# Block sums kept in PSUM, the gate's convolution in two PSUM banks, and another order of the FFN's units

## What is computed

```python
def causal_dwconv(u, buf, w, b):
    L, W = u.shape[1], w.shape[0]
    full = jnp.concatenate([buf.astype(u.dtype), u], axis=1)
    out = b + sum(full[:, j:j + L] * w[j] for j in range(W))
    return out, full[:, L:]

def conv_ffn(xn, buf, w_up, cw, cb, w_down):       # D_MODEL 1024, D_FF 2816, width 3
    up = xn @ w_up                                 # 1024 -> 5632, values and gates
    upc, new_buf = causal_dwconv(up, buf, cw, cb)
    val, gate = jnp.split(upc, 2, axis=-1)
    return (jax.nn.gelu(gate) * val) @ w_down, new_buf
```

## Time and profile before

| | |
|---|---|
| median of 3 runs | 1179.66 us (1179.26 to 1181.84) |
| the profiled execution's own time | 1180.18 us |
| its span, first to last instruction | 1178.4 us |
| TensorE busy | 1062.7 us, 90% |
| VectorE busy | 829.4 us, 70% |
| ScalarE busy | 519.5 us, 44% |
| GpSimd busy | 500.5 us, 42% |
| mean granted TensorE clock | 0.943 of full speed |
| pairs 0 to 4, without D | about 625 to 722 us |
| pairs 5 to 20, with D and D' | about 722 to 1110 us |

### The profile page before, as it was taken

One profiled execution on the slowest core, in us unless ns is written; L12 is line 12 of the kernel. 1 busy time (PEld: TensorE's weight loads), 2 busy tenths in 40 slices (PEclk: granted clock), 3 DMA queues, 4 the chain that ended last, 5 costly groups with the idle time before them and its releaser, 6 DMA issues.

```text
span 1178.4 us, 19870 instructions
## 1 busy us (share of the span) xinstructions
PE 1062.7 (90%) x7688; PEld 1031.2 (88%) x7688; DVE 829.4 (70%) x1258; ACT 519.5 (44%) x869; POOL 500.5 (42%) x320
## 2 busy tenths in 40 slices
PE   8999999999999999999997876888878887888885
PEld 8899999999999999999986866888878887888885
DVE  6885569565664648464567898877787788787964
ACT  6577873143435343242344444343433444344453
POOL 4243333432232323223444556555554565455630
PEclk9999999999999999999997988888988999898998
DMA  8533323775968677453311231222121222223036
GB/s 207 167 83 94 94 73 99 179 198 129 249 147 237 155 188 214 154 198 116 108 54 37 72 90 57 61 79 75 54 63 55 72 81 55 62 68 85 23 88 195
DMA packets 263267, 132.94 MB, mean 113 GB/s; under 512 B 82720, under 2 KB 257045, under 8 KB 262920
## 3 DMA queue, kind: packets, MB, share of 16 engines
q1 hardware_dynamic: 262966, 131.63, 41.2%
q10 hardware_dynamic: 210, 0.07, 0.0%
HBM read 104.17 MB, written 25.29 MB: 110 GB/s over the span
## 4 chain that ended last, share of the span: by engine, by line
PE 56%; DVE 15%; issue 10%; DMA 9%; ACT 4%; POOL 4%; SPq 1%; DVEq 0%; POOLq 0%; ACTq 0%
PE ring L2630 35%; PE ring L3035 8%; DMA f_stage<-in_w_up 8%; DVE conv L1781 5%; PE bank L3021 3%; DVE gl L2527 2%; PE bank L2872 2%; POOL f_lo L1192 2%; POOL wlo L1151 2%; DVE f_stage L2358 2%; ACT f_hi L1586 2%; DVE f_stage L2359 1%; PE bank L2676 1%; DVE f_stage L2366 1%; ACT gh L1682 1%
## 5 line engine op out<-in xcount | busy, mean ns | idle before, releaser
L1151 POOL TENSOR_TENSOR wlo<-stage,whi 128x1024 fp32r<-128x1024 f32 x78 | 200.3, 2568 | 400.1 <-ACT whi L1205 400.1
L2630 PE MATMUL ring<-x_split,whi 128*128 128x322 f32 (+2 forms) x1952 | 347.5, 300 | 0.0
L1192 POOL TENSOR_TENSOR f_lo<-f_stage,f_hi 128x512 fp32r<-128x512 f32 x154 | 224.9, 1469 | 212.8 <-ACT f_hi L1586 211.7
L2630 PEld LDWEIGHTS ring<-x_split,whi 128*128 128x128 f32 x1952 | 294.4, 189 | 8.9 <-issue 8.1
L2630 PE MATMUL ring<-x_split,wlo 128*128 128x256 f32 (+1 forms) x976 | 210.4, 297 | 0.0
L1586 ACT ACTIVATE f_hi<-f_stage 128x512 fp32r<-128x512 f32 x154 | 94.7, 627 | 208.1 <-DVE f_stage L2366 90.9
L2630 PEld LDWEIGHTS ring<-x_split,wlo 128*128 128x128 f32 x976 | 164.6, 189 | 0.0
L3035 PE MATMUL ring<-gh,f_hi 128*128 128x280 f32 (+1 forms) x316 | 84.2, 354 | 69.3 <-DVE resid L2532 59.1
L3035 PEld LDWEIGHTS ring<-gh,f_hi 128*128 128x128 f32 x316 | 63.9, 236 | 74.5 <-DVE resid L2532 62.9
L1205 ACT ACTIVATE whi<-stage 128x1024 fp32r<-128x1024 f32 x79 | 83.3, 1054 | 81.5 <-PE ring L2630 70.6
L3021 PE MATMUL bank<-fx_T,f_hi 128*128 128x290 f32 x308 | 96.5, 313 | 22.3 <-ACT sum_one L1645 11.8
(11 more groups left out here) (423 smaller groups left out, 2266.6 us busy)
## 6 DMA issues: line engine op xcount, KB each, us to landing
stage<-in_w_in SPq DMA_DIRECT2D x56, 512.0 KB, 4.2
f_stage<-in_w_up SPq DMA_DIRECT2D x44, 512.0 KB, 5.2
d_stage<-in_w_down SPq DMA_DIRECT2D x40, 256.0 KB, 2.8
stage<-in_w_branch_a SPq DMA_DIRECT2D x8, 512.0 KB, 3.6
c_sample<-in_state_mlstm_C SPq DMA_DIRECT2D x16, 256.0 KB, 6.6
out_s_mlstm_C<-c_sample SPq DMA_DIRECT2D x16, 256.0 KB, 2.4
stage<-in_w_branch_b SPq DMA_DIRECT2D x8, 512.0 KB, 3.7
stage<-in_w_out SPq DMA_DIRECT2D x8, 512.0 KB, 3.6
```

The costliest lines, as they stand in the source:

```text
L1151: pool.tensor_tensor(spaced(wlo[:, slot]), packed(stage[:, slot, 0:n]), spaced(whi[:, slot]).bitcast(F32), ALU.subtract).then_inc(w_lo, 1)
L1192: pool.tensor_tensor(in_blocks(flo[n % RING], key), packed(piece(key)), in_blocks(fhi[n % RING], key).bitcast(F32), ALU.subtract).then_inc ...
L2630: last = pe.matmul(of(z, t0 or -2, t1), w[:, kk * WS:kk * WS + P], x_, start=kk == 0 and m == 0, stop=kk == kn - 1 and m == 2)
```

## The change

**Sums in place.** The sums of partial products are no longer made in SBUF tiles: VectorE adds the SBUF copy of one part onto the PSUM accumulator of the other and scales from there. A pair uses four banks for its accumulators (one of two alternating banks A for B11, T2, T3, T4; one bank B for B21; one bank C for T1 and B22), with no double buffering of B and C.

**Gate in PSUM.** The gate's convolution, its gelu and the product with the values stand in the two banks that this frees (`cv[1]`, `sample_product`); the values' convolution stays in SBUF (`val_taps`). The hi and lo parts of the product are each made by two instructions (512 and 64 columns).

**History.** The copy of the samples' history into `up` moves from VectorE to ScalarE (`history`).

**Order.** TensorE's units, and with them all the other engines' work, stand in another order; the product of pair i-1 is made in pass i and no longer pair i-2's. D and D' share `wide[1]` as before.

```diff
 def weight_order():
     for i in range(NPAIR):
         yield "B11", i
-        yield "B21", i
+        yield "T1", i
+        if d:
+            yield "D", *d
         if i:
             yield "T4", i - 1
-        if d:
-            yield "D", *d
         yield "T2", i
-        if i:
-            yield "B22", i - 1
-        yield "T1", i
+        yield "B21", i
+        yield "B22", i
         if d:
             yield "D", d[0], d[1] + 1
         yield "T3", i
...
-        acc_banks = ((bank[:, 0], bank[:, 1], bank[:, 2]), (bank[:, 3], ring[:, 0, 0], ring[:, 0, 1]))
+        pool_ = bank[:, :, :].rearrange("p h t -> p (h t)")
+        cv = (val_taps[:, 0:CV_N], pool_[:, 0:CV_N])
+        sample_product = pool_[:, CV_N:CV_N + TD - SEQ]
+        acc_a = (bank[:, 2, 0:QT], bank[:, 3, 0:QT])
+        acc_b, acc_c = ring[:, 0, 0, 0:QT], ring[:, 0, 1, 0:QT]
...
             def load_pair(i):
                 if i >= 2:
-                    sp.wait_ge(piece_split, split_done("B22", i - 2))
+                    sp.wait_ge(piece_split, split_done("T4", i - 2))
...
+            def history(i, j):
+                act.activation(grouped(up[:, j, US0:UW_F - UG], UG)[:, :, 0:FW - 1], hist[:, :, ft:ft + UPT + 1:UPT], ACT.Copy
...
-            def first_sum(i):
-                tt(s_one[:, 0:QS], s_one[:, 0:QS], acc(i, 1)[:, 0:QS], ALU.add).then_inc(c11_added, 1)
-            def first_scaled(i):
-                tt(up[:, 0, 0:QS], s_one[:, 0:QS], rbc[:, 0:QS], ALU.mult).then_inc(c11_scaled, 1)
+            def sum_one_one(i):
+                b = acc(i, "B21")[:, 0:QS]
+                tt(b, s_one[:, 0:QS], b, ALU.add).then_inc(sum_added, 1)
+                tt(up[:, 0, 0:QS], b, rbc[:, 0:QS], ALU.mult).then_inc(sum_scaled, 1)
+            def sum_one_two(i):
+                c = acc(i, "B22")[:, 0:QS]
+                tt(c, s_two[:, 0:QS], c, ALU.add).then_inc(sum_added, 1)
+                tt(up[:, 1, 0:QS], c, rbc[:, 0:QS], ALU.mult).then_inc(sum_scaled, 1)
+            def sum_two_two(i):
+                tt(b, s_five[:, :], acc(i, "T3"), ALU.add).then_inc(sum_added, 1)
+                second_half(i, 1, b)
...
             def product(i):
-                st(tt(grouped(pr[:, SEQ:TD], LS), grouped(cv[:, 0, US0:US0 + UG * NB], UG)[:, :, 0:LS],
-                tt(pr[:, 0:SEQ], cv[:, 0, 0:SEQ], cv[:, 1, 0:SEQ], ALU.mult).then_inc(prod_done, 1)
+                st(tt(grouped(sample_product, LS), sample_conv(val_taps[:, :]), sample_conv(cv[1]), ALU.mult))
+                tt(cv[1][:, 0:SEQ], cv[0][:, 0:SEQ], cv[1][:, 0:SEQ], ALU.mult).then_inc(prod_done, 1)
...
             for i in range(NPAIR):
-                if i >= 2:
-                    product(i - 2)
+                if before:
+                    down_evict(before[0], before[1] + 1)
...
-                    pe.wait_ge(c21_scaled, i - 1)
-                up_product("B11", i, 0)
+                    pe.wait_ge(sum_scaled, scaled(i - 2, "C21"))
+                up_product("B11", i, True)
+                    pe.wait_ge(sum_scaled, scaled(i - 1, "C12"))
+                up_product("T1", i, True)
+                    pe.wait_ge(sum_added, added(i - 1, "C22"))
+                    up_product("T4", i - 1, False)
                 pe.wait_ge(part_copied, parts(i, 1))
+                    pe.wait_ge(sum_scaled, scaled(i - 1, "C22"))
+                up_product("B21", i, True)
+                pe.wait_ge(part_copied, parts(i, 2))
+                up_product("B22", i, False)
```

More of the change, by code:

```diff
@@ L290, in parts, with added, scaled @@
     return 3 * i + n
+def added(i, block):
+    return 3 * i + {"C11": 1, "C12": 2, "C22": 3}[block]
+def scaled(i, block):
+    return 4 * i + {"C11": 1, "C12": 2, "C22": 3, "C21": 4}[block]
 class Chain:
@@ L490, in hybrid_layer @@
         up = sb("up", [P, 2, UW_F], r)
[L491 to L497, removed]
+        r += 8 * UW_F
+        s_one, s_two, s_five = sb("sum_one", [P, QT], r), sb("sum_two", [P, QT], r + 1184), sb("part_five", [P, QT], r + 2 * 1184)
+        r += 3 * 1184
+        val_taps = sb("val_taps", [P, CV_N + 4], r)
+        r += 4 * CV_N + 5888
         dst = [sb(f"d_stage{s}", [P, QN], r + 4 * QN * s) for s in range(2)]
@@ L1654, in third_part, with part_five @@
-            def third_part(i):
-                act.wait_ge(tile_done, unit_done("T3", i))
+                    act.wait_ge(sum_added, added(i - 1, "C11"))
+                act.activation(s_one[:, 0:QS], acc(i, "B11")[:, 0:QS], ACT.Copy).then_inc(part_copied, 1)
+            def part_five(i):
+                act.wait_ge(tile_done, unit_done("T1", i))
+                if i:
+                    act.wait_ge(sum_added, added(i - 1, "C22"))
+                act.activation(s_five[:, :], acc(i, "T1"), ACT.Copy).then_inc(part_copied, 1)
@@ L1722, in _ @@
             i, g0, g1 = NPAIR - 1, GROUPS - 2, GROUPS - 1
+            first_tap(i, 1)
             ahead("D", g0, 0)
-            product_hi(i - 1)
+            gelu(i)
             ahead("T4", i)
             first_tap(i, 0)
-            ahead("B22", i)
-            first_tap(i, 1)
             ahead("D", g0, 1)
-            gelu(i)
             ahead("D", g0, 2)
@@ new lines, in second_half @@
+            def second_half(i, j, z):
+                st(tt(up[:, j, QS:US0], z[:, 0:UH_F], rtwo[:, 0:UH_F], ALU.mult))
+                ins = tt(sample_rows(up[:, j])[:, :, FW - 1:], grouped(z[:, UH_F:QT], LS), grouped(rtwo[:, UH_F:QT], LS),
+                         ALU.mult)
+                ins.then_inc(sum_scaled, 1)
+                dve.wait_ge(sum_scaled, scaled(i, "C22" if j else "C21"))
+                last_rows(i, j)
+            def sum_two_two(i):
+                b = acc(i, "B21")
+                dve.wait_ge(part_copied, parts(i, 2))
+                dve.wait_ge(tile_done, unit_done("T3", i))
+                dve.wait_ge(sum_scaled, scaled(i, "C12"))
+                tt(b, s_five[:, :], acc(i, "T3"), ALU.add).then_inc(sum_added, 1)
+                dve.wait_ge(sum_added, added(i, "C22"))
+                second_half(i, 1, b)
@@ L3079, in _ @@
             down_product(g0, 0)
-            pe.wait_ge(part_copied, parts(i, 3))
-            up_product("T4", i, 0, False)
-            pe.wait_ge(c22_added, i + 1)
-            up_product("B22", i, 2, False)
-            pe.wait_ge(c21_scaled, i)
-            pe.wait_ge(c11_added, i)
+            pe.wait_ge(sum_added, added(i, "C22"))
+            up_product("T4", i, False)
+            pe.wait_ge(sum_scaled, scaled(i, "C22"))
             down_product(g0, 1)
-            pe.wait_ge(c11_added, i + 1)
-            pe.wait_ge(c12_added, i + 1)
+            pe.wait_ge(sum_scaled, scaled(i, "C21"))
             down_product(g0, 2)
```

213 lines of the change are left out of this document (88 added, 125 removed).

## The result

The changed kernel takes 1109.53 us (median of 4 runs, 1107.44 to 1112.07) against 1179.61 before: ratio 0.9403, 95% interval 0.9379 to 0.9427. That is 70 us less; the forecast was 109 us less (1071).

A forecast was written before the change was run, and what follows sets the result against it. It took VectorE's late eviction of D, stalling TensorE, as the bound. 16 pairs from 24.0 to 18.0 us save 96, five others 13: 109 off 1180.2 gives 1071 us, range 1050 to 1122.

The forecast's parts named there:

- the half clock of D': TensorE's D' unit, slowed to clock 0.50 behind its stall for the eviction, up to 2.6 us; expected back at full clock.
- Four banks are enough: PSUM accumulators of a pair: loops through single banks take less than 17.7 us, so no bank holds TensorE up.
- writing PSUM: Rival, chance 0.06 for slower: seven VectorE instructions per pair write PSUM dearly; 1143 us at a doubling, 1215 at 1.2 each.
- VectorE's two waits for a split piece: VectorE idle in front of 2389 (1.2 us) and 2396 (about 0.4) until GpSimd has split a piece: 1.6 per pair.
- Weights come in time: The next pair's weight loads, issued at 13.6 us, make about 20, when VectorE wants them at 19.8.
- the waits for GpSimd grow: In VectorE's pass, waits for GpSimd go from 2.0 to 2.7 us per pair, plus 0.6 for the fourth weight sum.
- The upper bound of 6.3: Six VectorE instructions reading two SBUF tiles each wait out most of a GpSimd operation: 20.8 us per pair, 1129 us.
- the lock fills what was freed: Rival, chance 0.15: VectorE's two-SBUF-input instructions and GpSimd's exclude each other; pass 19.5 to 20.8 us, 1102 to 1129.
- the case that carried the forecast: Pairs with D take 17.7 to 19.5 us, 1052 to 1102 us in all; chance 0.70, 0.20 of it TensorE alone.
- The rival of the clock: Rival, chance 0.06: stalls of 3.4 to 3.9 us at T1 bring clock 0.5 behind them; 22.8 us per pair, 1161 us.
- 6.0 each, 90: Saving in the pairs with D: each goes from 24.0 to 18.0 us.
- The list of savings, mean by mean: VectorE work removed per pair, from old mean durations: scaling, product, lo part and history, 4.9 of 19.1 us.

The follow-up runs named there:

- lo_zero: The changed kernel with GpSimd writing zeros for the lo parts of the FFN weights instead of subtracting two SBUF tiles: 1047.23 us.
- round_product: The changed kernel with ScalarE's hi part of the product moved behind the roundings of the next pair's T2, B21 and B22: 1063.33 us.
- sums_sbuf: The changed kernel with the three sums back in SBUF tiles, and C11, C12 and half of C22 scaled from two SBUF tiles: 1121.05 us.
- before_lo_zero: The kernel before the change, with GpSimd writing zeros for the lo parts of the FFN weights: 1090.14 us.
- order_alone: The changed kernel with sums, gate and product back in SBUF and the history copied by VectorE, keeping the new order: 1133.37 us.

## Why the prediction was right, and where its size was off

**Right.** The eviction is no longer what TensorE waits for; the half clock of D' is gone (some of it now stands behind T1); what is left stands before T1, on 2496. Four banks are enough: where VectorE is not the bound (lo_zero, round_product) TensorE has no gap, so no wait for a bank costs anything. Operands in PSUM take the times of their like, and writing PSUM costs next to nothing: the three sums take 449, 456 and 455 ns into PSUM, and 441, 446 and 446 into SBUF (sums_sbuf). VectorE's two waits for a split piece came nearly as worked out: 1.4 and 0.4 us per pair, 1.8 against the 1.6 of the sum. (The 1.3 of GpSimd in that sum is not in the earlier trace rows, whose mean is 1.46; the changed kernel's trace has 1.31 at 845.91.) Weights come in time.

**The mis-sized term** is "the waits for GpSimd grow": 2.0 scaled with GpSimd's busy share to 2.7, and 0.6 for 2396, 3.3 together. Measured from the rows above: 0.97 on 2396, 1.10 on 2381 and on 2382, 1.02 on 2389 and twice 0.97 on the values' taps make 6.1. The pass closes with it: 12.5 bare with handovers, 1.8 of waits and 6.1 of lock are 20.4. A busy share says how often an engine is found at work by one that comes at random; here both engines are released by the same few events, have several instructions queued, and take turns until one queue is empty. The upper bound of 6.3 was nearly the case that came, so the rival "the lock fills what was freed" (19.5 to 20.8 per pair, 1102 to 1129) was the true one, at 0.15; I had argued against it that of two in a row only one waits, which held in the old kernel (2358 and 2359) and in the new one does not. That 1109.5 lies in the range 1050 to 1122 is therefore owed to its upper end, drawn to take in most of this rival; the case that carried the forecast, 17.7 to 19.5 per pair, did not come. The rival of the clock had its price from stalls of 3.4 and more, but 2.4 was followed by the half clock too, as was, in the kernel before, the 2.73 of the earlier trace rows at 1096.74 (0.50 behind it); it cost nothing, since VectorE was the bound.

**By stretches**, from the intervals of gelu: the pairs with D gave 54 us in 15 intervals instead of 6.0 each, 90; the four before them 15 instead of 10 (the last of them, 21.7 to 16.2, has a D pair's beginning in it); the last two lost 1.5. The first gelu comes 7.2 us earlier, and from the last gelu to the end 3.9 are lost, where the sum had 0.

**Right for the wrong reason.** The list of savings, mean by mean, made 4.9 us from PSUM and history. With the order given, sums, gate and history bring back 0.3, 0.1 and 0 us per pair with D. The means of the old kernel held waits that belong to the place of an instruction, not to it: taken off one, they turn up on the next one that reads two SBUF tiles while GpSimd still has pieces queued. That the pair became shorter by 3.1 of its 3.6 us is due to the order, of which I had priced only the waits of TensorE.

VectorE's own account says the same. The lock took 6.6 us per pair before (the long rows less their times in before_lo_zero) and takes 6.1 now, so the change moved it and hardly made it smaller. VectorE's busy time fell from 19.1 to 18.2 us per pair, its idle time from 4.9 to 2.2. Most of that idle time was waits for ScalarE and TensorE: the three in the earlier trace rows with 15.7, 13.7 and 19.0 us, and this one, none of which the changed kernel has in its stretch:

```profile
DVE sum_three L2493 <- ACT sum_three L1659: 20.0, 16, 1.3
```

**Open.** Within order_alone, the order of TensorE's units, that of the three other engines and the four banks were not tried apart; which of them freed VectorE of its waits is not shown. Nor were the pairs without D taken further, 15.1 us in the changed kernel and 13.9 in round_product against 11.3 of matmuls.
